# Merging nearly empty gate tiles and taking the first norm's statistics under the modulation columns, in a two-block transformer kernel

## The reference

```python
def modulate(x, g, mod, i):
    return rms_norm(x, g) * (1 + mod[:, :, i + 1]) + mod[:, :, i]

mod_l = (jax.nn.silu(c) @ ada_w[layer] + ada_b[layer]).reshape(batch, 1, N_MOD, D_MODEL)
mod_c = (jax.nn.silu(c_ctx) @ ada_w[layer] + ada_b[layer]).reshape(1, 1, N_MOD, D_MODEL)
h_l = modulate(x, norm1_g[layer], mod_l, 0)
h_c = modulate(ctx, norm1_g[layer], mod_c, 0)
```

## Time and profile before

| | us |
|---|---|
| median of 3 runs | 4483.39 |
| the profiled execution, its own time | 4480.93 |
| its span (first to last instruction) | 4478.7 |
| TensorE matmul busy (PE) | 3972.2 |
| DVE busy | 2246.4 |
| GpSimd busy (POOL) | 1284.0 |
| ScalarE busy (ACT) | 793.7 |

### The profile page before, as it was taken

How to read it: one execution, slowest core, us unless ns; L and a number is a source line. 1 busy time by engine, 2 the same in 40 slices (tenths; PEclk the granted TensorE clock), 3 DMA queues, 4 the chain that set the end, 5 groups by cost and what they waited for, 6 DMA issues and landing times.

```text
span 4478.7 us, 45446 instructions
## 1 busy us (share of the span) xinstructions
PE 3972.2 (89%) x18934; PEld 3231.3 (72%) x18934; DVE 2246.4 (50%) x3669; ACT 793.7 (18%) x1470; POOL 1284.0 (29%) x522
## 2 busy tenths in 40 slices
PE   7976888999997899999999647999999997658998
PEld 5964468999984578888878425788788785346886
DVE  4734557876644452343455264634633472457334
ACT  3024332101124320100011221100100121311001
POOL 1310002333330044444444000444344341003443
PEclk9989899999998999999999657999999997569999
DMA  5400002343320022232222000222222221002222
GB/s 195 151 29 1 1 15 88 124 127 125 106 71 10 19 87 97 97 109 99 96 84 98 19 0 15 84 95 99 87 94 99 90 92 45 0 1 71 99 94 85
DMA packets 103695, 335.61 MB, mean 75 GB/s; under 512 B 11426, under 2 KB 11586, under 8 KB 103236
## 3 DMA queue, kind: packets, MB, share of 16 engines
q1 hardware_dynamic: 78192, 282.29, 18.8%
q10 hardware_dynamic: 25300, 50.43, 3.6%
HBM read 330.58 MB, written 2.10 MB: 74 GB/s over the span
## 4 chain that ended last, share of the span: by engine, by line
PE 57%; DVE 8%; ACT 3%; issue 1%; DVEq 0%; ACTq 0%
PE PS L497 48%; PE PS L979 1%; DVE XH L778 1%; PE PS L890 1%; PE PS L1835 1%; DVE arena L1935 0%; DVE arena L1933 0%; PE PS L499 0%; PE PS L1595 0%; PE PS L1596 0%; DVE H_r L655 0%; PE PS L1701 0%; DVEq L319 0%; PE PS L1838 0%; PE PS L970 0%
## 5 line engine op out<-in xcount | busy, mean ns | idle before, releaser
L497 PE MATMUL PS<-arena_r,ring_hi 128*128 128x512 f32 (+1 forms) x6272 | 2118.1, 376 | 98.2 <-DVE H_r L655 94.8
L2164 POOL TENSOR_TENSOR ring_r<-ring,ring_hi 128x1024 fp32r<-128x1024 f32 x518 | 1283.8, 2480 | 3159.7 <-DVE ring_hi L337 3159.7
L497 PE MATMUL PS<-arena_r,ring_r 128*128 128x512 f32 (+1 forms) x4800 | 1799.7, 375 | 0.0
L497 PEld LDWEIGHTS PS<-arena_r,ring_hi 128*128 128x128 f32 x6272 | 1177.4, 189 | 282.4 <-issue 99.1
L497 PE MATMUL PS<-H_r,ring_hi 128*128 128x512 f32 (+1 forms) x3328 | 1249.4, 375 | 0.0
L497 PEld LDWEIGHTS PS<-arena_r,ring_r 128*128 128x128 f32 x4800 | 906.7, 189 | 133.5
L497 PEld LDWEIGHTS PS<-H_r,ring_hi 128*128 128x128 f32 x3328 | 632.0, 190 | 93.8 <-issue 0.5
L337 DVE CAST ring_hi<-ring 128x1024 fp32r<-128x1024 f32 x518 | 503.3, 974 | 277.9 <-DMA ring<-weights_dram 277.3
L1482 DVE SCALAR_TENSOR_TENSOR arena<-arena,PS 128x512 f32<-128x512 f32 x88 | 60.5, 688 | 449.1 <-PE PS L497 449.1
L1478 ACT ACTIVATE arena<-PS 128x512 f32<-128x512 f32 x88 | 52.6, 598 | 1073.1 <-PE PS L497 1073.1
L1093 DVE SCALAR_TENSOR_TENSOR XH<-PS,mods,XH 128x256 f32<-128x256 f32 (+1 forms) x144 | 68.5, 523 | 208.5 <-PE PS L497 208.5
(11 more groups left out here) (340 smaller groups left out, 3456.9 us busy)
## 6 DMA issues: line engine op xcount, KB each, us to landing
ring<-weights_dram SPq DMA_DIRECT2D x534, 512.0 KB, 3.3
rstd<-ada_later_dram ACTq DMA_DIRECT2D x54, 256.0 KB, 2.7
mean<-ada_later_dram ACTq DMA_DIRECT2D x53, 256.0 KB, 2.8
ada_extra<-ada_later_dram ACTq DMA_DIRECT2D x53, 256.0 KB, 2.9
XH<-xT_dram ACTq DMA_DIRECT2D x1, 3072.0 KB, 22.9
out_dram<-XH SPq DMA_DIRECT2D x8, 256.0 KB, 2.0
con<-second_dram ACTq DMA_DIRECT2D x1, 1536.0 KB
con<-first_dram ACTq DMA_DIRECT2D x1, 1280.0 KB, 8.1
```

What stands on the lines that cost most here:

```text
L497: ins = pe.matmul(PS[:, o.bank, 0:hi - lo], w[:, 0, :], x, **flags)
L2164: nc.gpsimd.tensor_tensor(ring_lo[:, slot, :, :], ring[:, slot, :, :], ring_hi[:, slot, :, :].bitcast(F32), ALU.subtract).then_inc(lo_read ...
```

## The change

Four edits. (1) `gi` and `gf` become one tile `gates` with its rows at partitions 0, 32, 64 and 96, copied out in two pieces; `be`, `de` and `gl` become one tile with rows at 0, 32 and 64, copied out in three. (2) The first norm's squares, sums, roots and the multiplication by the root move into the `ada` stage. The squares are added by DVE (14 additions), and TensorE has one matmul with the matrix of ones for each segment instead of 8, put in front of the last of the four groups of modulation columns. Only the affine step on ScalarE and the splits stay behind the barrier. (3) The loads of `crow` and `first` are issued at the end of the `ada` stage, and Silu of the rows runs behind the affine steps; DVE waits for it at the first half column. (4) Slabs 9, 11, 13 and 15 are issued by ScalarE between the squares (the last one behind the roots), not by SyncE. Before the first matmuls behind the barrier DVE casts one slab instead of three, and then one after every second k instead of every third.

```diff
-    s += ftiles("gi", (0, P)) + ftiles("gf", (0, P))
+    s += ftiles("gates", (0, P))
...
-                s += ftiles(f"be{l}", (0, P)) + ftiles(f"de{l}", (0, P))
-                s += ftiles(w, (2576, 2832)) + ftiles(w, (3088, 3344)) + ftiles(f"gl{l}", (0, P))
+                s += ftiles(f"gates{l}", (0, P)) + ftiles(w, (2576, 2832)) + ftiles(w, (3088, 3344))
...
+ACT_SLABS = range(9, RAW_SLABS, 2)
...
+            if n == 0:
+                dve.wait_ge(rows_silu.sem, 1)
...
+        def rows_dve_to(pieces, first):
+
+            def ev(eng, ps, lo, hi):
+                for dst, at, n in pieces:
+                    ins = nc.vector.tensor_copy(dst[0:n, lo - first:hi - first], ps[at:at + n])
+                return ins
+            return ev
...
-        def norm_act(act, segs, eps, centred, affine, summed):
+        def norm_act(act, segs, eps, centred, affine):
+            inverse_roots(act, segs, eps, centred)
+            scaled_act(act, segs, affine)
+
+        def scaled_act(act, segs, affine):
+            for k in range(KD):
+                for lo, hi in segs:
+                    act.wait_ge(norm_ready.sem, norm_ready.next("act"))
+                    affine(act, k, lo, hi).then_inc(affine_done.sem, 1)
...
-            if not summed:
-                for lo, hi in segs:
-                    for k in range(KD):
-                        nc.scalar.activation(tmp_sq[:, k, lo:hi], X[:, k, lo:hi], ACT.Square).then_inc(sq_ready.sem, 1)
-
-                nc.scalar.activation(small[:, 159:160], V("one"), ACT.Ln)
...
+        def fetch_slab(act, n):
+
+            used, count = Weights.used[n - RING]
+            act.wait_ge(used.sem, count)
+            act.dma_start(ring[:, n % RING, :, :].rearrange("p a b -> p (a b)"), w_d[n]).then_inc(slab_loaded[n % RING].sem, 16)
+
+        def first_squares_act(act, segs):
+            for k in range(KD):
+                if k % 3 == 0:
+                    fetch_slab(act, ACT_SLABS[k // 3])
+                for lo, hi in segs:
+                    nc.scalar.activation(tmp_sq[:, k, lo:hi], X[:, k, lo:hi], ACT.Square).then_inc(sq_ready.sem, 1)
+
+            nc.scalar.activation(small[:, 159:160], V("one"), ACT.Ln)
+
+        def first_sums_pe(pe, segs):
+            for i, (lo, hi) in enumerate(segs):
+                pe.wait_ge(first_acc.sem, first_acc.at("pe", (KD - 2) * len(segs) + i))
+                pe.matmul(PS[:, i, 0:hi - lo], C("ones"), tmp_sq[:, 0, lo:hi], start=True, stop=True).then_inc(sum_ready.sem, 1)
+
+        def first_squares_dve(dve, segs):
+            n = len(segs)
+            for k in range(1, KD):
+                for i, (lo, hi) in enumerate(segs):
+                    dve.wait_ge(sq_ready.sem, sq_ready.at("dve", k * n + i))
+                    if k >= 2:
+                        dve.wait_ge(first_acc.sem, first_acc.at("dve", (k - 2) * n + i))
+                    nc.vector.tensor_tensor(tmp_sq[:, 0, lo:hi], tmp_sq[:, 0, lo:hi], tmp_sq[:, k, lo:hi], ALU.add).then_inc(first_acc.sem, 1)
+
+        def first_norm_dve(dve, segs):
+            split_up_to(dve, RAW_SLABS + 1)
             for k in range(KD):
                 for lo, hi in segs:
-                    act.wait_ge(norm_ready.sem, norm_ready.next("act"))
-                    affine(act, k, lo, hi).then_inc(affine_done.sem, 1)
-
-        def norm_pe(pe, segs):
-            for i, (lo, hi) in enumerate(segs):
-                for k in range(KD):
-                    pe.wait_ge(sq_ready.sem, sq_ready.next("pe"))
-                    ins = pe.matmul(PS[:, i, 0:hi - lo], C("ones"), tmp_sq[:, k, lo:hi], start=(k == 0), stop=(k == KD - 1))
-                ins.then_inc(sum_ready.sem, 1)
+                    dve.wait_ge(affine_done.sem, affine_done.next("dve"))
+                    split_input(dve, H, False, k, lo, hi)
+                split_ahead(dve, k, 2)
...
-        ada_rows = area(0, ADA_FIRST * P)
+        ada_rows = area(8192, ADA_FIRST * P)
...
-            act.dma_start(con2[:, 0:FIRST_AT["cos128"]], first_d[:, 0:FIRST_AT["cos128"]]).then_inc(loaded.sem, 16)
             act.dma_start(X[:], xT_d.rearrange("(k p) t -> p k t", p=P)).then_inc(loaded.sem, 16)
-            for s in range(2):
-                act.dma_start(silu_rows[s], crow_d[s]).then_inc(rows_loaded.sem, 16)
             act.wait_ge(vec_loaded.sem, 16)
             nc.scalar.activation(cs[:, :, 0], V("c", 0, 8), ACT.Silu)
             nc.scalar.activation(cs[:, :, 1], V("c_ctx", 0, 8), ACT.Silu).then_inc(silu_c.sem, 1)
-            act.wait_ge(rows_loaded.sem, 32)
-            for s in range(2):
-                nc.scalar.activation(silu_rows[s], silu_rows[s], ACT.Silu)
+            act.wait_ge(loaded.sem, 32)
+            first_squares_act(act, ALL)
+            inverse_roots(act, ALL, "eps1", False)
+            fetch_slab(act, ACT_SLABS[3])
             for i in range(N_ADA):
                 act.wait_ge(ada_out.sem, i + 1)
                 nc.scalar.activation(ada_rows[0:2, 512 * i:512 * i + 512], PS[0:2, 2 + i, :], ACT.Copy).then_inc(ada_row.sem, 1)
...
+        def later_loads(act):
+
+            act.wait_ge(ada_done.sem, 1)
+            for s in range(2):
+                act.dma_start(silu_rows[s], crow_d[s]).then_inc(rows_loaded.sem, 16)
+            act.dma_start(con2[:, 0:FIRST_AT["cos128"]], first_d[:, 0:FIRST_AT["cos128"]]).then_inc(first_loaded.sem, 16)
+
+        def silu_rows_act(act):
+
+            act.wait_ge(rows_loaded.sem, 32)
+            for s in range(2):
+                ins = nc.scalar.activation(silu_rows[s], silu_rows[s], ACT.Silu)
+            ins.then_inc(rows_silu.sem, 1)
...
             for i in range(N_ADA):
+                if i == N_ADA - 1:
+                    pe.wait_ge(loaded.sem, 32)
+                    first_sums_pe(pe, ALL)
...
-            pe.wait_ge(loaded.sem, 48)
             pe.wait_ge(ada_row.sem, N_ADA)
             for m in range(ADA_FIRST):
-                ins = pe.transpose(PS[:, 0, 2 * m:2 * m + 2], ada_rows[0:2, P * m:P * m + P], C("ident")[0:2, 0:2])
+                ins = pe.transpose(PS[:, 6, 2 * m:2 * m + 2], ada_rows[0:2, P * m:P * m + P], C("ident")[0:2, 0:2])
...
-            dve.wait_ge(loaded.sem, 48)
+            dve.wait_ge(loaded.sem, 32)
+            sum_ready.advance("dve", len(ALL))
+            first_squares_dve(dve, ALL)
+            dve.wait_ge(std_ready.sem, std_ready.next("dve", len(ALL)))
+            for k in range(KD):
+                for i, (lo, hi) in enumerate(ALL):
+                    nc.vector.tensor_tensor(H[:, k, lo:hi], X[:, k, lo:hi], root(i)[:, 0:hi - lo], ALU.mult).then_inc(norm_ready.sem, 1)
             dve.wait_ge(ada_done.sem, 1)
...
-            t += [ftile(x_h, ALL, "dve", copy_dve(to(d))) for d in (kb, gi, gf)]
+            t += [ftile(x_h, ALL, "dve", copy_dve(to(kb))), ftile(x_h, ALL, "dve", rows_dve_to([(gi, 0, 64), (gf, 64, 64)], 0))]
...
+            dve.wait_ge(first_loaded.sem, 16)
...
-                + [zp[:, m, :] for m in range(4)] + [be, de, qg, kg, rg[:, 0, :], rg[:, 1, :], gl]
+                + [zp[:, m, :] for m in range(4)] + [None, qg, kg, rg[:, 0, :], rg[:, 1, :]]
...
-                elif i < 20 or i in (24, 25):
+                elif i < 20 or i in (23, 24):
                     t.append(ftile(x_x, LAT, "act", func_act(to_lat(d), ACT.Silu)))
+                elif i == 20:
+                    t.append(ftile(x_x, LAT, "dve", rows_dve_to([(be, 0, 8), (de, 32, 8), (gl, 64, 16)], CTX)))
...
             def dve_fn(e):
-                if before:
-                    before(e)
                 norm_dve(e, segs, centred, last)
-            add(None if summed else lambda e: norm_pe(e, segs),
-                lambda e: norm_act(e, segs, eps, centred, affine, summed), dve_fn, barrier=last)
+            add(None, lambda e: norm_act(e, segs, eps, centred, affine), dve_fn, barrier=last)
...
-        add(ada_pe, ada_act, ada_dve)
-        add_norm(ALL, "eps1", False, modulate(0, 0), summed=False, before=lambda e: split_up_to(e, RAW_SLABS + 3))
-        add_gemm(ab_plan())
+        add(ada_pe, lambda e: (ada_act(e), later_loads(e)), ada_dve)
+        add(None, lambda e: scaled_act(e, ALL, modulate(0, 0)), lambda e: first_norm_dve(e, ALL), barrier=False)
+        split_tiles_of(ALL)
+        Norms.affine += KD * len(ALL)
+        add_gemm(ab_plan(), before=silu_rows_act)
...
+                if n in ACT_SLABS:
+                    continue
...
-    mats = dict(ada0=a["ada_w"][0], ab=ab, gi=spread(ab, [(2048, 4, 0), (2056, 4, 32)]),
-                gf=spread(ab, [(2052, 4, 0), (2060, 4, 32)]), abo=a["ab_w_out"][0], cw=a["c_w_in"][0], co=a["c_w_out"][0])
+    mats = dict(ada0=a["ada_w"][0], ab=ab, gates=spread(ab, [(2048, 4, 0), (2056, 4, 32), (2052, 4, 64), (2060, 4, 96)]), abo=a["ab_w_out"][0], cw=a["c_w_in"][0], co=a["c_w_out"][0])
```

(24 more changed lines are left out.)

## The result

| | median us (lowest to highest, runs) | ratio to before (95%) |
|---|---|---|
| before | 4482.93 (4481.84 to 4484.00, 4) | |
| after | 4431.09 (4423.82 to 4435.97, 4) | 0.9883 (0.987 to 0.9895) |

The change saves 51.8 us, 1.2%. The profiled execution took 4435.97 us (span 4434.2), and the sum, made on the profiled execution of before, gave 4435.5. It is also the slowest of the four: 4435.97, 4431.29, 4430.90 and 4423.82 at mean clocks of 0.920, 0.921, 0.922 and 0.924.

The account below looks back on a forecast made before the run. The prediction took TensorE as the bound, busy 3972.2 of 4478.7 us. Gains of 30.2 + 15.1 + 0.1 = 45.4 us took the profiled 4480.93 to 4435.5, and 2.5 more for the runs gave 4438, range 4431 to 4448.

Parts of the forecast that it names:

- the sum: Whole kernel: 30.2 + 15.1 + 0.1 = 45.4 us off the profiled 4480.93 gives 4435.5; 2.5 more gives 4438.
- Part 1: Merged tiles in the `ab` GEMM and two `in_plan` calls: 8.42 + 2 x 2 x 5.44 = 30.2 us saved, bounds 28 to 31.
- Rival C: In `in_plan`, merged copies make DVE late, 1.4 x 2 us, giving 4441; chance 0.03.
- Part 2: Norm moved from behind the barrier: first split matmul 4.9 to 5.1 us after it, gain 15.1, bounds 12 to 16.8.
- rival D: From its first unit in the `ab` GEMM, TensorE stays at half clock; 4620 us if throughout that GEMM; chance 0.02.
- Part 3: `ada` stage: loads moved away against the norm's added work; gain 0.1 us, bounds 3 gained to 5 lost.
- The 2 us wait for slab 15: `ada` stage: slab 15, issued behind the roots, lands at 41.2; TensorE, needing it at about 39.3, waits 2 us.
- rival B: The start gives more: first, no wait at slab 15; second, casts unstretched; 4438 - 4.7 = 4433 us, chance 0.06.
- the `in_plan` term: In each of two `in_plan` calls three tiles become one, at 5.44 us per tile: 2 x 2 x 5.44.

Follow-up runs that it names:

- e1: The kernel before with only the tiles merged; median 4452.48 us, ratio 0.9931 to the kernel before.
- e6: The changed kernel with `first` loaded ahead of X and `crow` behind it, as in the kernel before; 4433.15 us in one run.
- e4: The changed kernel run again with no edit; median 4432.44 us, ratio 0.9889 to the kernel before.
- e12: The changed kernel run once more with no edit; median 4431.02 us, ratio 0.9886 to the kernel before.
- e2: The changed kernel with the merged tiles undone, leaving the norm and load edits; median 4466.49 us, ratio 0.9962 to the kernel before.
- e8: The changed kernel with SyncE issuing all slabs, half the multiplications and slab 16's cast before the barrier, late loads behind the first affine; 4425.55 us, ratio 0.9873.

## Why the prediction came out as it did

**Part 1 was right in its mechanism.** 30.2 us forecast, 30.2 measured in `e1`, with the two distances unchanged; that the median of `e1` agrees to 0.1 us is luck, at an interval of 6 to either side. By stage `ab` gave 8.3 (forecast 8.42) and the two `in_plan` stages 12.5 and 11.0 (10.88 each), and over the three executions of the changed kernel 10.6 to 12.5. Rival C did not occur.

**Part 2 was right.** First split matmul 4.9 to 5.1 us behind the barrier forecast, 5.0 measured, with the stretched cast in the place named. 15.1 us forecast; `ab` lost 23.6, less 8.4 for the tile: 15.2. The 14 matmuls at 0.33 became 18 at 0.32, until 55.7. PE waited nowhere in the first unit, and the clock was 1.00 behind it: rival D did not occur.

**Part 3 was undersized, with three of its steps wrong.** 0.1 us forecast, 0.9 to 1.5 measured (44.5 to 45.1 for 46.0), within the bounds. Products began at 6.29, not 8.5: slab 0 took 7.2 to landing with `first` in flight beside it, 7.1 again in `e6`, and 5.0 without (1.17 to 6.2). X landed at 21.1, not 19, which moved the squares but not the sums (DVE's last addition ended at 31.3, TensorE's third group at 31.7). The 2 us wait for slab 15 did not occur: I let the DMA wait for the Exps, while ScalarE's sequencer issued it before they ran. The first and the last let the products end 3 us earlier (40.2 for 43.0); of that the stage got one, since DVE's multiplications (44.1, forecast 45.0) were then the last. That is rival B's first half without its second.

**The step that failed is the sum: it put the stages that the change doesn't touch at nothing, without a reason, and sized part 3 and the `in_plan` term too small.** The changed stages gave 47.1 to 49.3 us, 48.4 on average over `after`, `e4` and `e12`, where 45.4 was forecast. Of the 3.0 more, part 3 is 1.1 (1.2 measured for 0.1), `in_plan` 1.7 (23.5 for 21.8) and `ab` 0.2. The stages left alone moved by -5.2 to +7.8 us in the same executions, more than all of that. The sum also carried one profiled execution to the runs by adding 2.5. But that execution, at 4480.93, is below all 27 others of before (4481.8 to 4490.9), and the median of after lies 4.9 below its profiled one, not above. So some 4 of the 6.9 us missed come from outside the changed stages, and no trace shows where, since only one run of each set has one. What such a stage can do by itself is shown by windows of two stages with the same instructions (start:end, us, busy us and count of PE, PEld, DVE, ACT, POOL; clock, DMA share, GB/s). The mLSTM stage, before:

```profile
296.30:413.10 116.80, 91.68 (x438) 65.49 (x438) 54.80 (x161) 41.65 (x137) 0.00 (x0) 0.85 0.00 1
```

After, then the stage with the `out`, MLP 0 and `c` GEMMs, whole and its first 30 us:

```profile
271.50:385.00 113.50, 88.46 (x438) 63.17 (x438) 54.74 (x161) 41.61 (x137) 0.00 (x0) 0.88 0.00 1
601.60:1322.30 720.70, 693.91 (x3829) 675.20 (x3830) 485.85 (x822) 121.51 (x236) 223.46 (x83) 0.98 0.32 102
```

`e12`, the same kernel:

```profile
270.80:383.10 112.30, 87.19 (x438) 62.47 (x438) 54.81 (x160) 41.62 (x137) 0.00 (x0) 0.90 0.00 1
598.40:1312.30 713.90, 687.65 (x3814) 670.95 (x3815) 488.11 (x823) 121.79 (x237) 222.65 (x83) 0.98 0.33 103
```

The shorter the mLSTM stage, the higher its clock (`e2`: 119.0 us at 0.82). Measured in the same way it took 112 to 116 us in all eleven traces of kernels with both halves of the change, and 116.8 in the one of before. In the other stage most of the 7 us hang on one moment. After, then `e12`, PE:

```profile
601.53 1.73 PE L1053 MATMUL PS<-scratch,arena 128*128 128x128 f32 x8 [2.03 <-ACT arena L1115]
604.03 2.05 PE L1053 MATMUL PS<-scratch,arena 128*128 128x128 f32 x8 [0.78 <-ACT arena L1115]
606.77 6.29 PE L1040 MATMUL PS<-arena 128*64 128x512 f32 x8 [0.69 <-ACT arena L1115]
```

```profile
598.64 1.13 PE L1053 MATMUL PS<-scratch,arena 128*128 128x128 f32 x8 [2.04 <-ACT arena L1115]
600.55 1.13 PE L1053 MATMUL PS<-scratch,arena 128*128 128x128 f32 x8 [0.78 <-ACT arena L1115]
602.37 3.65 PE L1040 MATMUL PS<-arena 128*64 128x512 f32 x8 [0.69 <-ACT arena L1115]
```

The pauses are the same to 0.01 us, the instructions too; in the one execution the clock fell to half within 0.4 us behind the first of them, in the other it stayed. The first split matmul of the stage comes 14.6 us behind the first of these lines in the one and 10.5 in the other, and with the next matmuls, 0.32 apart for 0.175, 5.4 of the 6.8 us are lost. `e4` fell at the same place (719.7 for the stage); the kernel before stayed up (713.80). Whether the change makes such falls likelier or rarer for this kernel, and so whether the 4 us are the change's or chance, stays open. With a single trace of before the shorter mLSTM stage is a hint, no more: the twelve runs of after reach from 4423.8 to 4439.4 (by median 51.8, 50.2 and 53.7 under before in three sets), 27 of before from 4481.8 to 4490.9.

## What to carry to other kernels

What a tile costs in a stretch where TensorE never waits is the distance between the copies that end neighbouring tiles, and it can be subtracted: 8.3 us came out for 8.42 in `ab`, 10.6 to 12.5 for 10.88 in a stage of 500 to 950 us. For work moved under another engine's stretch, count on for each of the moved pieces what stands behind it, as the sums behind slab 11 here, since this decides whether it fits. A load that is not needed early is worth moving for the transfers behind which it stands: here it delayed the slabs. Before a range goes below 0.3%, see by how much stages that the change leaves alone differ between executions, and give that a term.

## What the hardware showed beyond expectation

- ScalarE's queue issued a DMA (34.36) while the table load in front of two activations was running (34.34 to 35.62) and before these ran (35.64, 36.06), though the program has it behind them. The slab's DMA waited for no semaphore of these activations, so its place behind them in the program was no bound for its start.
- Not the cast alone is stretched by POOL's run: beside a run of about 2.4 us a two-operand subtraction on DVE took 2.62 in place of 0.56. In `e8` a step on 8 columns took 1.22 in place of 0.17. The trace agrees with the Trainium skill, "SBUF — State Buffer", section "Who interferes with whom": an instruction of DVE with two SBUF inputs contends with one of GpSimd that reads SBUF.
- Behind the same pause (2.03 and 2.04 us) TensorE fell to half clock in one execution of a kernel and not in another, which cost 5.4 us. Equal pauses behind equal work don't decide whether it falls.
